# A third mixer's input projections in three passes of high and low parts instead of one pass of full fp32

## The reference, cut to what matters

```python
hn = rms_norm_2(h, mix_norm_g[l])
proj = jnp.einsum('bld,dp->blp', hn, w_in[l])      # 272 x 1024 by 1024 x 3072
q, k, v, cx, cb, cc = jnp.split(proj, splits, axis=-1)   # six parts of 512 columns
attn = diff_attention_group(q, k, v, ..., cos, sin)       # 4 heads, two softmaxes each, then a norm
conv = cb * centred_depthwise_conv(cc * cx, conv_w[l])
h = h + jnp.einsum('blm,md->bld', concat(attn, conv), w_out[l])
h = h + expert_choice_ffn(rms_norm_2(h, ffn_norm_g[l]), w_router[l], w_gate[l], w_up[l], w_down[l])
```

## Time and profile before

| | |
|---|---|
| median of 3 runs | 1846.42 us (1845.08 to 1852.51) |
| the profiled execution | 1844.83 us, of which the span of the trace is 1843.5 us |
| TensorE busy | 1666.2 us, 90% of the span |
| VectorE, ScalarE, GpSimd busy | 652.7, 362.9, 32.3 us |
| DMA | 577.32 MB, 313 GB/s on the mean |
| the third mixer's projections and attention | from 725.40 to 845.56 us of the span |

### The profile page before, as it was taken

How to read it: one execution, slowest core, us unless ns; L and a number is a source line. 1 busy time by engine, 2 the same in 40 slices (tenths; PEclk the granted TensorE clock), 3 DMA queues, 4 the chain that set the end, 5 groups by cost and what they waited for, 6 DMA issues and landing times.

```text
span 1843.5 us, 20831 instructions
## 1 busy us (share of the span) xinstructions
PE 1666.2 (90%) x8861; PEld 1005.6 (55%) x8861; DVE 652.7 (35%) x1264; ACT 362.9 (20%) x632; POOL 32.3 (2%) x39
## 2 busy tenths in 40 slices
PE   4989999999999999999999978898788887789777
PEld 3776899998699998578533322233222222222223
DVE  6667487646957553362311101011010010110102
ACT  2223443433433342141100000000000000000001
POOL 0101000000000000100010000000000000000000
PEclk8999999999999999999899989999999999999899
DMA  9655377637656453223599999999999999999996
GB/s 395 250 223 205 137 269 280 229 138 280 251 206 248 185 185 137 98 85 137 203 415 418 416 430 431 428 429 432 430 430 428 431 424 430 431 428 430 431 431 264
DMA packets 43549, 577.32 MB, mean 313 GB/s; under 512 B 4785, under 2 KB 5954, under 8 KB 7234
## 3 DMA queue, kind: packets, MB, share of 16 engines
q1 hardware_dynamic: 43458, 576.00, 76.2%
HBM read 574.93 MB, written 1.05 MB: 312 GB/s over the span
## 4 chain that ended last, share of the span: by engine, by line
PE 70%; DMA 22%; DVE 5%; ACT 1%; issue 1%; SPq 0%; DVEq 0%; ACTq 0%
DMA RING_T<-in_w_up 21%; PE P L1063 18%; PE P L434 13%; PE P L1088 6%; PE P L773 4%; PE P L772 4%; PE P L771 4%; PE P L443 3%; PE P L792 2%; PE P L791 2%; PE P L790 2%; PE P L1041 2%; DVE RING_T L1663 2%; PE P L1105 2%; DMA RING_T<-in_ada_w 1%; PE P L1064 1%
## 5 line engine op out<-in xcount | busy, mean ns | idle before, releaser
L1063 PE MATMUL P<-RING_T,SCR 128*34 128x512 f32 x1008 | 480.9, 633 | 115.1 <-DMA RING_T<-in_w_up 115.0
L1064 PE MATMUL P<-RING_T,SCR 128*34 128x512 f32 x992 | 474.8, 635 | 0.0
L1063 PEld LDWEIGHTS P<-RING_T,SCR 128*34 128x34 f32 x1008 | 114.1, 118 | 429.7 <-issue 429.1
L2205 DVE TENSOR_TENSOR SCR<-P,SCR 34x512 f32<-34x512 f32 x64 | 44.3, 692 | 591.8 <-ACT SCR L1546 591.8
L1088 PE MATMUL P<-RING_T,SCR 128*34 128x512 f32 x512 | 227.7, 594 | 9.6 <-DMA RING_T<-in_w_down 9.6
L1089 PE MATMUL P<-RING_T,SCR 128*34 128x512 f32 x512 | 227.7, 594 | 0.0
L434 PE MATMUL P<-HWC,RING_T 128*128 128x256 f32 (+1 forms) x800 | 184.9, 388 | 3.2 <-ACT SCR L1154 3.0
L771 PE MATMUL P<-SCF 128*128 128x256 f32 x640 | 181.1, 283 | 0.0
L772 PE MATMUL P<-SCF 128*128 128x256 f32 x640 | 181.1, 283 | 0.0
L773 PE MATMUL P<-SCF 128*128 128x256 f32 x640 | 181.1, 283 | 0.0
L434 PEld LDWEIGHTS P<-HWC,RING_T 128*128 128x128 f32 x800 | 151.8, 191 | 34.4 <-issue 5.6
(11 more groups left out here) (266 smaller groups left out, 1841.4 us busy)
## 6 DMA issues: line engine op xcount, KB each, us to landing
RING_T<-in_w_gate SPq DMA_DIRECT2D x63, 2048.0 KB, 16.7
RING_T<-in_w_down SPq DMA_DIRECT2D x63, 2048.0 KB, 13.1
RING_T<-in_w_up SPq DMA_DIRECT2D x62, 2048.0 KB, 12.3
RING_T<-in_ada_w SPq DMA_DIRECT2D x24, 2048.0 KB, 11.8
RING_T<-in_ffn_w SPq DMA_DIRECT2D x22, 2048.0 KB, 8.1
RING_T<-in_ffn_w SPq DMA_DIRECT2D x22, 1024.0 KB, 4.9
RING_T<-in_ab_w_in SPq DMA_DIRECT2D x7, 2048.0 KB, 17.5
RING_T<-in_w_in SPq DMA_DIRECT2D x6, 2048.0 KB, 8.1
```

Source lines behind the costliest of these rows:

```text
L1063: pe.matmul(u.t[0:CAP, :], xs, wg.v(KC, 512)[:, c, :], start=c == 0, stop=c == KC - 1)
L1064: ins = pe.matmul(u.t[64:64 + CAP, :], xs, wu.v(KC, 512)[:, c, :], start=c == 0, stop=c == KC - 1)
```

## The change

The six parts' weights are split into 24 pieces of 128 x 1024 (`SPLIT_UNITS`), each what one chunk needs; a piece of v2 holds two of the eight row blocks. ScalarE writes the high part into one of six buffers (`NSPLIT`), VectorE writes the low part over the weights in the ring. Buffer n is free again when the chunk that used piece n - 6 is done. The first six pieces are split at the end of the second FFN, the others at fixed places in ScalarE's and VectorE's order. The normed H is split too: ScalarE copies it into `HH`, VectorE writes the rest into `HL`. The four q2 chunks become one block, `first`, that takes the tiles of H one by one for all four. The rotary matmuls are regrouped. The weights of five of the parts lie in DRAM so that a piece is contiguous; the loads keep their size, number and order. Some buffers share space: attention output and CX lie in MIX, and the scratch rows are shorter.

```diff
+    def first():
...
+        uses = [pe_bank(nc, k, ("q2", j)) for j in range(4)]
+        units = [parts("q2", j) for j in range(4)]
+        pe_busy(nc, k, uses[0], 8)
+        for c in range(KC):
+            pe.wait_ge(s["dhh"], c + 1)
+            for u, (uh, ul) in zip(uses, units):
+                pe.matmul(u.t[:, 0:L], uh[:, c * 128:(c + 1) * 128], v.HH[:, c, :], start=c == 0, stop=False)
+                pe.matmul(u.t[:, 0:L], ul[:, c * 128:(c + 1) * 128], v.HH[:, c, :], start=False, stop=False)
+        for j, (u, (uh, ul)) in enumerate(zip(uses, units)):
+            for c in range(KC):
+                if j == 0:
+                    pe.wait_ge(s["dhl"], c + 1)
+                ins = pe.matmul(u.t[:, 0:L], uh[:, c * 128:(c + 1) * 128], v.HL[:, c, :], start=False, stop=c == KC - 1)
+            ins.then_inc(u.full, 1)
...
-    def chunk(name, j, hn=None):
+    def chunk(name, j):
+        u = pe_bank(nc, k, (name, j))
+        uh, ul = parts(name, j)
+        for c in range(KC):
+            wh, wl = uh[:, c * 128:(c + 1) * 128], ul[:, c * 128:(c + 1) * 128]
+            pe.matmul(u.t[:, 0:L], wh, v.HH[:, c, :], start=c == 0, stop=False)
+            pe.matmul(u.t[:, 0:L], wh, v.HL[:, c, :], start=False, stop=False)
+            ins = pe.matmul(u.t[:, 0:L], wl, v.HH[:, c, :], start=False, stop=c == KC - 1)
...
+    first()
+    chunk("k2", 0)
+    rope("q2", v.Q, 0)
+    rope("q2", v.Q, 1)
+    chunk("k2", 1)
+    rope("q2", v.Q, 2)
+    rope("q2", v.Q, 3)
+    for j in (2, 3):
         chunk("k2", j)
-        rope("k2", v.K, j - 1) if j else rope("q2", v.Q, 3)
+        rope("k2", v.K, j - 2)
...
+class ActSplit:
...
+    def upto(self, n):
+        nc, k = self.nc, self.k
+        while self.n < n:
+            name, z = SPLIT_UNITS[self.n]
+            w = k.ring[name]
+            if z == 0:
+                nc.scalar.wait_ge(w.sem, w.n)
+            if self.n >= NSPLIT:
+                nc.scalar.wait_ge(*k.split_left[self.n - NSPLIT])
+            nc.scalar.activation(k.split_hi[self.n % NSPLIT], w.t[:, z * 1024:(z + 1) * 1024], ACT.Copy).then_inc(k.sem["split_hi"], 1)
+            self.n += 1
...
+class DveSplit:
...
+    def upto(self, n):
+        nc, k = self.nc, self.k
+        while self.n < n:
+            name, z = SPLIT_UNITS[self.n]
+            w, a, b = k.ring[name], z * 1024, (z + 1) * 1024
+            nc.vector.wait_ge(k.sem["split_hi"], self.n + 1)
+            nc.vector.tensor_tensor(w.r[:, a:b], w.t[:, a:b], k.split_hi[self.n % NSPLIT].bitcast(F32),
+                                    ALU.subtract).then_inc(k.sem["split_lo"], 1)
+            self.n += 1
...
+    for c in range(KC):
+        dve.wait_ge(s["dhh"], c + 1)
+        dve.tensor_tensor(v.HL[:, c, :], k.H[:, c, :], v.HH[:, c, :].bitcast(F32), ALU.subtract).then_inc(s["dhl"], 1)
...
     attend(0)
     attend(1)
+    split.upto(16)
     attend(2)
+    split.upto(18)
     subln(0)
+    split.upto(19)
     attend(3)
     gated(0)
+    split.upto(20)
     subln(1)
     gated(1)
+    split.upto(22)
     convolve(0)
     gated(2)
+    split.upto(23)
     convolve(1)
     subln(2)
     gated(3)
+    split.upto(24)
```

More of the change, by code:

```diff
@@ L375, with __init__ @@
 class DiffViews:
[L376 to L379, removed]
+    def __init__(self, t, r, s):
+        self.LM = t.take(4)
+        self.MIX = t.take(KC, L)
+        self.OT, self.CX = self.MIX[:, 0:4, :], self.MIX[:, 4:8, :]
+        self.mx, self.sm = [t.take(3, 2) for _ in range(4)], [t.take(3, 2) for _ in range(4)]
+        self.UH, self.HH = r.take(4, 1024), r.take(KC, L)
+        self.bufs = [s.take(4, L), s.take(4, L)]
         self.Q, self.K = s.take(4, L), s.take(4, L)
@@ L383, in __init__ @@
         self.AT = s.take(2, 3, L)
[L384 to L387, removed]
+        self.U = s.take(4, L + 2)
+        assert t.at <= 2600 and s.at <= 21440 - 2600 - 4096 - KC * L, (t.at, s.at)
 class ExpertViews:
@@ L890, in rope @@
         pe.matmul(u.t[:, 0:L], k.cc("rot64"), src[:, j, :], start=True, stop=True).then_inc(u.full, 1)
[L892 to L896, removed]
+    first()
[6 more added lines that the diff above has]
+    for j in (2, 3):
         chunk("k2", j)
-        rope("k2", v.K, j - 1) if j else rope("q2", v.Q, 3)
-    w2 = ring["v2"]
-    pe.wait_ge(w2.sem, w2.n)
+        rope("k2", v.K, j - 2)
     def rows(i):
-        u = pe_rows(nc, k, ("v2", i), w2.v(KC, 512), k.H, *TILES[i])
+        r, m = TILES[i]
+        u = pe_bank(nc, k, ("v2", i))
+        for z in range(4):
+            uh, ul = parts("v2", z)
+            for c in (2 * z, 2 * z + 1):
+                o, x, y = u.t[0:m, :], v.HH[:, c, r:r + m], v.HL[:, c, r:r + m]
+                wh, wl = uh[:, (c % 2) * 512:(c % 2 + 1) * 512], ul[:, (c % 2) * 512:(c % 2 + 1) * 512]
+                pe.matmul(o, x, wh, start=c == 0, stop=False)
+                pe.matmul(o, x, wl, start=False, stop=False)
+                ins = pe.matmul(o, y, wh, start=False, stop=c == KC - 1)
+        ins.then_inc(u.full, 1)
         if i == 2:
-            w2.left = (u.full, u.n)
+            for z in range(4):
+                k.split_left[SPLIT_AT["v2", z]] = (u.full, u.n)
+            ring["v2"].left = (u.full, u.n)
     def attend(hd):
@@ L1577, in scalar_program @@
 def scalar_program(nc, k):
-    high = [ActHigh(nc, k, layer) for layer in range(2)]
+    high, split = [ActHigh(nc, k, layer) for layer in range(2)], ActSplit(nc, k)
     act_ab(nc, k, high[0])
-    act_ffn(nc, k, 0, high[0])
+    act_ffn(nc, k, 0, high[0], split)
     act_cd(nc, k, high[1])
-    act_ffn(nc, k, 1, high[1])
-    act_diff(nc, k)
+    act_ffn(nc, k, 1, high[1], split)
+    act_diff(nc, k, split)
     act_experts(nc, k)
@@ L1968, in dve_ffn @@
             dve_ada(nc, k, *extra.pop(0))
+    if layer:
+        split.upto(NSPLIT)
     gate = k.gate(layer, 1)
@@ L2265, in vector_program @@
 def vector_program(nc, k):
-    low = [DveLow(nc, k, layer) for layer in range(2)]
+    low, split = [DveLow(nc, k, layer) for layer in range(2)], DveSplit(nc, k)
     dve_ab(nc, k, low[0])
-    dve_ffn(nc, k, 0, low[0])
+    dve_ffn(nc, k, 0, low[0], split)
     dve_cd(nc, k, low[1])
-    dve_ffn(nc, k, 1, low[1])
-    dve_diff(nc, k)
+    dve_ffn(nc, k, 1, low[1], split)
+    dve_diff(nc, k, split)
     dve_experts(nc, k)
```

95 lines of the change are left out of this document (74 added, 21 removed).

## The result

The kernel after takes 1831.7 us (median of 5 runs, 1830.43 to 1835.16), the one before beside it 1846.42 us (5 runs, 1842.32 to 1854.66): ratio 0.9913 [0.9895, 0.9930]. In a second comparison it was 1830.83 us (4 runs) against 1848.16 (7 runs), ratio 0.9903 [0.9880, 0.9926]. The forecast was 1828.0, with a range up to 1834. The ratios are estimates over all runs, not quotients of the medians; the medians by themselves lie 14.7 and 17.3 us apart.

A forecast was written before the change was run, and what follows sets the result against it. TensorE bounds the third mixer, and the expert weight stream, whose start is tied to TensorE, the second half. 21.1 - 0.3 - 0.5 - 0.4 - 1.2 = 18.7 us off 1846.42 gives 1827.7, say 1828; range 1821.5 to 1834.

The forecast's parts named there:

- the additive rival: Projection matmuls: 13 ns come on top of streaming with every fp32r matmul, time 1830.5 to 1831 us; chance 18%.
- The pitch: Time from one projection matmul's start to the next: 120 ns at 272 columns, 216 ns at 512; gain 21.1 us.
- they look like a floor set by the weight load: Projection matmuls: the 13 ns above streaming at 256 columns aren't a constant, so 272 columns take the floor of 120 ns.
- The end of the FFN: Second FFN's end: six splits on VectorE make residual adds, squares and sums of squares 0.3 us later.
- The start of the mixer: Third mixer's start: H goes through ScalarE's copy before TensorE may begin, 0.5 us later.
- ScalarE late for `pv(0)`: In the mixer, through splits 16 and 17 ScalarE reaches the copies behind `turn_p(0)` about 0.4 us late; charged 0.4 us.
- VectorE's lag: Mixer from head 2 on: VectorE has 38.5 to 39.2 us of work for 37.1; cost 0 to 4 us, taken as 1.2.
- The rival that made VectorE the bound: Mixer's second half: late gates make TensorE wait, 3 to 8 us of the gain lost, 1831 to 1835 us; chance 14%.
- The clock moved with the work: After the router: TensorE's clock falls near 876 and rises near 894 us, the later distances staying as before.
- The rival in which it gives 8 us back, or takes as much: Router stage: the half-speed stretch shifts or vanishes, up to 8 us more gain (1820 to 1825) or about 8 lost; chance 10%.
- Slower: Projection chunks: fp32r at 272 columns takes over 153 ns; at two cycles a column about 1878 us; chance 4%.
- no change: Whole kernel: the end is set by the expert weight stream, which starts elsewhere, so nothing is gained; chance 1%.

The follow-up runs named there:

- e8_pitch2: Changed kernel with further groups of 24 added matmuls between mixer and output projection (more fp32r sizes, fewer stationary columns, bf16, accumulating fp32r): 1874.89 us.
- e2_vector2: Changed kernel with two extra VectorE subtractions of 320 columns ahead of each of the last ten low parts: 1830.77 us.
- e2_vector4: Changed kernel with four extra VectorE subtractions of 320 columns ahead of each of the last ten low parts: 1845.17 us.
- the second profile: The changed kernel run and profiled again without an edit: 1830.83 us, ratio 0.9903 to the kernel before.
- e1_pitch: Changed kernel with 24 groups of 24 added matmuls (fp32r at many sizes, four groups in fp32) before the output projection: 1930.94 us.
- e7_clock2: Changed kernel with nine dummy matmul pairs in the holes of the router's stage: 1832.26 us, ratio 0.9924 to the kernel before.

## Why the prediction came out as it did

The mechanism was right: fp32's two records of two cycles a column give way to three matmuls of one, TensorE sets the pace, and what it gains ahead of the first expert reaches the end. The sum was 18.7 us where 16.6 were gained, and errors in it partly cancelled. That 1831.7 us lies in the range is owed to the range taking in the additive rival; the forecast's own 1828.0 lies below all five runs of the first comparison (from 1830.43).

**The pitch was mis-sized, which made the gain 3.9 us too large.** The step that failed is "they look like a floor set by the weight load". At 272 columns a matmul takes 125.5 ns and not 120, at 512 it takes 228.8 (in v2 itself 16.86 us by 72, 234) and not 216. A chunk is 3.01 us instead of 2.88 and saves 0.66 instead of 0.79, twenty save 13.2 instead of 15.8; v2 takes 16.86 instead of 15.55 and saves 4.0 instead of 5.3. Together 17.2 instead of 21.1. I had taken one size, 256 columns, and two types, and gave the difference between the types to the load. The additive rival, "the 13 ns come with every fp32r matmul", was nearly right above 240 columns (126.7 and 226.7 ns forecast), and its time of 1830.5 to 1831 is next to the two medians, 1831.7 and 1830.83. The rival had "For it: no row at another size", and one at 512 columns would have settled it; with the two about equally open, 18% was too little. What the floor does instead, at 112 ns, e8_pitch2 shows.

The Trainium skill, "TensorE: Matmul & The Clock Gate", section "Back-to-back issue gap", gives N/2.4 + 2.5 ns. The bf16 groups agree with it (115.8 against 115.8 ns at 272 columns), the fp32r groups don't (125.5, and 228.8 against 215.8 at 512); for fp32r the measurement decides. The same page, section "LDWEIGHTS (loading the stationary operand)", gives 107 ns for 128 columns; the measured floor is 112 ns, but it is no guide to 272 columns.

**The end of the FFN: 0.3 us, measured 0.2.** From the table load to the first residual addition it was 9.04 us, now 9.21; TensorE's wait for the squares grew from 0.49 to 0.7 us. Timeline:

```profile
710.84 4.63 DVE L2044 TENSOR_TENSOR RING_R<-RING_T,SCF 128x1024 fp32r<-128x1024 f32 x4 [1.16 <-ACT SCF L1435]
...
716.52 1.22 DVE L2044 TENSOR_TENSOR RING_R<-RING_T,CB_R 128x1024 fp32r<-128x1024 f32 x1
717.66 1.65 DVE L1819 SCALAR_TENSOR_TENSOR X<-P,MOD,X 128x256 f32<-128x256 f32 x4
```

Four splits take 4.63 us, and each starts some 1.14 us behind the last, as taken over from the earlier trace rows.

**The start of the mixer: 0.5 us, measured 0.5.** The norm's first tile is written from 727.80, the first matmul starts at 728.82 (timelines): 1.02 us, before 0.55.

```profile
727.80 3.39 DVE L1809 SCALAR_TENSOR_TENSOR HWC<-X,VC,RS 128x272 f32<-128x272 f32 x8
```

**ScalarE late for `pv(0)`: 0.4 us, measured 0.** No such wait is among TensorE's. That the slower chunks gave ScalarE the time is possible and not shown.

**VectorE's lag: 1.2 us, measured 0.1.** The wait ahead of the output projection is 0.9 instead of 0.8 us. The work was sized about right: 38.5 to 39.2 us forecast, 38.08 measured. What was wrong is the time for it. The 37.1 us end some 6 us ahead of the mixer's end, and e2_vector2 and e2_vector4 show some 8 us of room. Of these the slower chunks gave about 1.3 us (ten by 0.13), so the lag would have been small at 120 ns too (an estimate). I charged 1.1 us for an overload that wasn't there, and by luck it made up for part of the error in the pitch. The rival that made VectorE the bound falls with it, and e2_vector4 shows at which point it would have been true: 8 us more work.

In sum 17.2 - 0.2 - 0.5 - 0.1 = 16.4 us, where 16.62 were measured; 0.2 stays unassigned.

**The clock moved with the work, roughly.** The fall was forecast near 876 and the rise near 894; measured were about 883 and 900, of which 2.8 us are the later table load. Counted from the first gather, the fall came 1 us ahead of it before and 1 us behind it after. The half speed lasted 17 us as before, and 14 in the second profile. The stage with the gathers takes 22.42 and 20.78 us in the two profiles, 21.75 in that of before. The rival in which it gives 8 us back, or takes as much, didn't happen in these two.

**Slower, and no change:** a matmul at 272 columns is 125.5 ns, far from the 153 ns at which the chunks would lose. And the stream starts 13.2 us earlier in the profile.

## What to carry to other kernels

When a price rests on one size, name the two formulas that both fit it (a floor and a constant), and see at which size they part; both ends belong into the range, with more weight on the unflattering one. Before charging for an engine that falls behind, count the time that it has up to the end of the stage; here it had some 8 us more than it needed, where a window that ended too early showed an overload. And where the effect is 1% and the rest of the program moves by nearly as much (11 and 3.5 us here), compare a stage between two events, which here repeats to 0.03 us, and use the totals only to see that the gain is kept.

## What the runs showed of the hardware

- A matmul in fp32r costs 12 to 16 ns above its streaming at 2.4 GHz from 240 to 512 columns (once 20, at 448), one in bf16 about 2.5 ns at 256 to 512 (e1_pitch, e8_pitch2). With 128 stationary columns fp32r doesn't go below some 112 ns (seen from 96 to 240 moving columns), with 112 stationary columns it takes 98 ns at 192.
- In e1_pitch the clock fell to 0.50 behind a stretch of short matmuls in which TensorE was busy 2.00 of 2.00 us, and with filling in the router's stage it fell behind 12.00 of 12.00 us (e7_clock2). The Trainium skill, "TensorE: Matmul & The Clock Gate", section "HAM oscillation — how this bites in real kernels", names idle gaps of TensorE as what brings it down. The falls in the kernels before and after come behind gaps, in these two runs there was none.
- The stream of the experts' weights took 924.9 to 935.9 us in twelve profiled executions of kernels that don't differ in it, and the work up to the second FFN's end 705.3 to 708.8.
